# The second layer's down projection in pairs of column tiles, with 6 of its 22 chunk pairs computed by seven block products in place of eight

## What is computed

```
SEQ = 256
D_MODEL = 2048
FFN_HIDDEN = ((-(-8 * D_MODEL // 3)) + 255) // 256 * 256      # 5632
def swiglu(xn, w_gate, w_up, w_down):
    return (jax.nn.silu(xn @ w_gate) * (xn @ w_up)) @ w_down
...
        x = x + swiglu(rms_norm(x, ffn_norm[layer]), w_gate[layer], w_up[layer], w_down[layer])
```

## Time and profile before

| | |
|---|---|
| three executions | 2115.74, 2116.29, 2118.04 us; median 2116.29 |
| the profiled execution: its own time, its span | 2115.71 us, 2113.9 us |
| mean granted TensorE clock, as a share of full speed | 0.999 |
| PE, DVE, ACT busy, share of the span | 100%, 65%, 47% |
| down projection of the second layer, first matmul to first matmul of its second column tile | 59.84 us |

### The profile page before, as it was taken

How to read it: one execution, slowest core, us unless ns; L and a number is a source line. 1 busy time by engine, 2 the same in 40 slices (tenths; PEclk the granted TensorE clock), 3 DMA queues, 4 the chain that set the end, 5 groups by cost and what they waited for, 6 DMA issues and landing times.

```text
span 2113.9 us, 27639 instructions
## 1 busy us (share of the span) xinstructions
PE 2103.6 (100%) x9321; PEld 1739.6 (82%) x9321; DVE 1375.7 (65%) x1879; ACT 996.8 (47%) x1249; POOL 77.5 (4%) x85
## 2 busy tenths in 40 slices
PE   9999999999999999999999999999999999999999
PEld 7788888888888888888888888888888888888887
DVE  5777667676666766565576776676776667664443
ACT  6555555444444444444455565454444444443433
POOL 0110011000000000000011000110000000000000
PEclk9999999999999999999999999999999999999999
DMA  8788666666666665556677774666666666655663
GB/s 277 225 250 254 209 208 199 182 191 199 197 195 181 191 203 182 191 186 207 193 229 248 231 221 152 203 197 198 180 194 202 192 185 189 199 185 201 210 211 136
DMA packets 235252, 427.16 MB, mean 202 GB/s; under 512 B 16176, under 2 KB 37808, under 8 KB 235184
## 3 DMA queue, kind: packets, MB, share of 16 engines
q1 hardware_dynamic: 232736, 422.07, 63.8%
q10 hardware_dynamic: 2448, 4.21, 0.6%
HBM read 410.23 MB, written 15.99 MB: 202 GB/s over the span
## 4 chain that ended last, share of the span: by engine, by line
PE 94%; DVE 2%; DMA 2%; issue 1%; ACT 1%; SPq 0%; POOL 0%; ACTq 0%; DVEq 0%
PE psum L623 30%; PE psum L626 30%; PE psum L624 30%; PE psum L677 1%; PE psum L691 1%; DVE w_lo L1088 1%; DMA block_dram<-turn_sb 1%; DMA w_raw<-in_ab_w_out 1%; DMA w_raw<-in_cd_w_out 1%; PE psum L643 0%; ACT w_hi L777 0%; DVE xt_lo L1164 0%; DMA w_raw<-in_ab_w_in 0%; SPq L509 0%; DMA x_res<-in_x 0%
## 5 line engine op out<-in xcount | busy, mean ns | idle before, releaser
L1088 DVE TENSOR_TENSOR w_lo<-w_raw,w_hi 128x1024 fp32r<-128x1024 f32 x759 | 906.5, 1200 | 619.0 <-ACT w_hi L777 613.5
L777 ACT ACTIVATE w_hi<-w_raw 128x1024 fp32r<-128x1024 f32 x759 | 786.0, 1040 | 933.9 <-PE psum L626 897.4
L623 PE MATMUL psum<-w_hi,xt_hi 128*128 128x512 f32 x2012 | 791.5, 393 | 3.0 <-ACT stage L874 3.0
L626 PE MATMUL psum<-w_hi,xt_lo 128*128 128x512 f32 x2012 | 783.9, 390 | 0.0
L624 PE MATMUL psum<-w_lo,xt_hi 128*128 128x512 f32 x2012 | 783.6, 389 | 0.0
L623 PEld LDWEIGHTS psum<-w_hi,xt_hi 128*128 128x128 f32 x2012 | 378.1, 188 | 81.6 <-DVE w_lo L1088 3.4
L626 PEld LDWEIGHTS psum<-w_hi,xt_lo 128*128 128x128 f32 x2012 | 378.1, 188 | 79.6
L624 PEld LDWEIGHTS psum<-w_lo,xt_hi 128*128 128x128 f32 x2012 | 378.3, 188 | 78.0
L623 PE MATMUL psum<-w_hi,ht_hi 128*128 128x512 f32 x960 | 377.7, 393 | 0.7 <-DVE stage L1121 0.7
L626 PE MATMUL psum<-w_hi,ht_lo 128*128 128x512 f32 x960 | 373.8, 389 | 0.0
L624 PE MATMUL psum<-w_lo,ht_hi 128*128 128x512 f32 x960 | 373.6, 389 | 0.0
(11 more groups left out here) (122 smaller groups left out, 614.9 us busy)
## 6 DMA issues: line engine op xcount, KB each, us to landing
w_raw<-in_w_gate SPq DMA_DIRECT2D x176, 512.0 KB, 3.6
w_raw<-in_w_up SPq DMA_DIRECT2D x176, 512.0 KB, 3.7
w_raw<-in_w_down SPq DMA_DIRECT2D x160, 512.0 KB, 4.1
w_raw<-in_cd_w_in SPq DMA_DIRECT2D x80, 512.0 KB, 4.4
w_raw<-in_ab_w_in SPq DMA_DIRECT2D x71, 512.0 KB, 4.4
w_raw<-in_ab_w_out SPq DMA_DIRECT2D x32, 512.0 KB, 4.2
w_raw<-in_cd_w_out SPq DMA_DIRECT2D x32, 512.0 KB, 3.7
block_dram<-turn_sb SPq DMA_DIRECT2D x18, 512.0 KB, 4.2
```

Source lines behind the costliest of these rows:

```text
L623: nc.tensor.matmul(acc, hi[:, chunk, ts], w_hi[:, slot, c, :], start=first and c == 0, stop=False)
L626: mm = nc.tensor.matmul(acc, lo[:, chunk, ts], w_hi[:, slot, c, :], start=False, stop=end)
L777: nc.scalar.activation(w_hi[:, slot, 0:n, :], w_raw[:, slot, 0:n, :], ACT.Copy).then_inc(hi_ready, 1)
L1088: nc.vector.tensor_tensor(w_lo[:, slot, 0:n, :], w_raw[:, slot, 0:n, :], w_hi[:, slot, 0:n, :].bitcast(F32), ALU.subtract).then_inc(lo_rea ...
```

## The change

The four column tiles of the second layer's down projection become two pairs, the twin tiles (`d` = 0, 1). Within a twin tile the units alternate between the two column tiles `j` = 0 and 1 at the same chunk pair `p`, up to pair 18; the last three pairs come tile by tile. A twin tile has 44 units, and no units of a single chunk are left. The loops over tiles are written out and no longer a hardware loop.

For six of the 22 pairs (`SEVEN`) the four blocks of activations (two token halves by two chunks) and the four blocks of weights (two chunks by two column tiles) are multiplied by the seven products of Strassen's method in Winograd's form. One such group is called **a seven** here. It takes the place of two units, and has 21 matmuls in place of 24. It needs:

- four sums of 128x128 blocks of activations: `row_sums` on DVE (5 operations) into `s_raw`, `rows_hi` on ACT into `s_hi`, and one subtraction on DVE into `s_lo`;
- four sums of 128x512 blocks of weights: 4 operations on DVE in `seven_operands` into `t_raw`, `sums_hi` twice on ACT into `t_hi_sb` (1024 columns each), and two subtractions on DVE into `t_lo_sb`;
- the upper unit (`a`) split as before, and of the lower unit (`b`) only its second chunk (`split_lower` on ACT, and one subtraction of 512 columns on DVE).

Three of the seven products use `w_hi`, `w_lo` or row sums alone (9 matmuls); four use `t_hi_sb` and `t_lo_sb` (12 matmuls), behind one wait for both halves (`tl_ready`). Products that go to one output are accumulated in the tile's own PSUM banks (`plain_bank`), those that go to several in four more banks (`seven_bank`). After the last seven of a twin tile, ACT copies one bank and DVE adds the four banks up with the residual (`combine`, 8 operations); the tile's own banks are added at its end (`output_add`).

```
+PAIRS = HC // 2
+SEVEN = (3, 6, 9, 12, 15, 18)
+PLAIN_END = 19
+TWIN_UNITS = [(j, p) for p in range(PLAIN_END) for j in range(2)]
+TWIN_UNITS += [(j, p) for j in range(2) for p in range(PLAIN_END, PAIRS)]
+TU = len(TWIN_UNITS)
+TWIN_END = [max(i for i, (tile, _) in enumerate(TWIN_UNITS) if tile == j) for j in range(2)]
+SEVEN_END = 2 * SEVEN[-1] + 1
...
+                def three(acc, a_hi, a_lo, b_hi, b_lo, start, stop=False):
+                    nc.tensor.matmul(acc, a_hi, b_hi, start=start, stop=False)
+                    nc.tensor.matmul(acc, a_hi, b_lo, start=False, stop=False)
+                    return nc.tensor.matmul(acc, a_lo, b_hi, start=False, stop=stop)
+                def own(acc, p, c, tok, b_hi, b_lo, start, stop=False):
+                    ts = slice(tok * P, tok * P + P)
+                    return three(acc, ht_hi[:, UC * p + c, ts], ht_lo[:, UC * p + c, ts], b_hi, b_lo, start, stop)
+                def seven_products(d, i, p):
+                    s = len(SEVEN) * d + SEVEN.index(p)
+                    first, last = p == SEVEN[0], p == SEVEN[-1]
+                    a, b = i % RING, (i + 1) % RING
...
+                    pe.wait_ge(lo_ready, twin_unit(d, i) + 1)
+                    own(seven_bank(d, 0), p, 0, 0, w_hi[:, a, 0, :], w_lo[:, a, 0, :], first, last)
+                    mm = own(plain_bank(d, 0, 0), p, 1, 0, w_hi[:, a, 1, :], w_lo[:, a, 1, :], False)
+                    mm.then_inc(unit_used, 1)
+                    pe.wait_ge(lo_ready, twin_unit(d, i + 1) + 1)
+                    pe.wait_ge(s_ready, s + 1)
+                    mm = three(plain_bank(d, 1, 0), s_hi[:, 3, :], s_lo[:, 3, :], w_hi[:, b, 1, :], w_lo[:, b, 1, :], False)
+                    mm.then_inc(unit_used, 1)
+                    pe.wait_ge(tl_ready, 2 * s + 2)
+                    three(seven_bank(d, 1), s_hi[:, 0, :], s_lo[:, 0, :], t_hi_sb[:, 0, :], t_lo_sb[:, 0, :], first, last)
+                    three(seven_bank(d, 3), s_hi[:, 2, :], s_lo[:, 2, :], t_hi_sb[:, 1, :], t_lo_sb[:, 1, :], first, last)
+                    three(seven_bank(d, 2), s_hi[:, 1, :], s_lo[:, 1, :], t_hi_sb[:, 2, :], t_lo_sb[:, 2, :], first, last)
+                    own(plain_bank(d, 0, 1), p, 1, 1, t_hi_sb[:, 3, :], t_lo_sb[:, 3, :], False).then_inc(seven_used, 1)
+                def plain_unit(d, i, j, p):
+                    if p == 0 and j == 0 and d:
+                        pe.wait_ge(combined, d)
+                    pe.wait_ge(lo_ready, twin_unit(d, i) + 1)
+                    for tok in range(TOK):
+                        for c in range(UC):
+                            mm = own(plain_bank(d, j, tok), p, c, tok, w_hi[:, i % RING, c, :], w_lo[:, i % RING, c, :],
+                                     p == 0 and c == 0, i == TWIN_END[j] and c == UC - 1)
...
+                    mm.then_inc(unit_used, 1)
+                if layer == 1:
+                    for d in range(XT // 2):
+                        for i, (j, p) in enumerate(TWIN_UNITS):
+                            if d == 0:
+                                pe.wait_ge(tile_split, split_count(1, "up", p))
+                            if p not in SEVEN:
+                                plain_unit(d, i, j, p)
+                            elif j == 0:
+                                seven_products(d, i, p)
...
+            def split_lower(u, slot):
+                act.wait_ge(w_loaded[slot], loads(u, slot))
+                act.wait_ge(unit_used, u - RING + 1)
+                nc.scalar.activation(w_hi[:, slot, 1, :], w_raw[:, slot, 1, :], ACT.Copy).then_inc(hi_ready, 1)
+            def sums_hi(s, half):
+                if s:
+                    act.wait_ge(seven_used, s)
+                act.wait_ge(t13_summed if half == 0 else t24_summed, s + 1)
+                nc.scalar.activation(t_hi_sb[:, 2 * half:2 * half + 2, :], t_raw[:, 2 * half:2 * half + 2, :],
+                                     ACT.Copy).then_inc(th_ready, 1)
+            def rows_hi(s):
+                if s:
+                    act.wait_ge(seven_used, s)
+                act.wait_ge(s_summed, s + 1)
+                nc.scalar.activation(s_hi[:], s_raw[:], ACT.Copy).then_inc(s_hi_ready, 1)
+            def twin_tiles():
+                for d in range(XT // 2):
+                    for i, (j, p) in enumerate(TWIN_UNITS):
+                        u = twin_unit(d, i)
+                        if p in SEVEN and j == 1:
+                            split_lower(u, i % RING)
+                        else:
+                            split(u, i % RING)
+                        if d == 0 and i == LEAD + 3:
+                            hidden_hi(1, HT - 1)
+                        if p in SEVEN and j == 0:
+                            rows_hi(len(SEVEN) * d + SEVEN.index(p))
+                        for half in range(2):
+                            before = i - 1 - half
+                            if before >= 0 and TWIN_UNITS[before][0] == 1 and TWIN_UNITS[before][1] in SEVEN:
+                                sums_hi(len(SEVEN) * d + SEVEN.index(TWIN_UNITS[before][1]), half)
+                        if i == SEVEN_END + LEAD:
+                            act.wait_ge(seven_used, len(SEVEN) * (d + 1))
+                            if d:
+                                act.wait_ge(x_combined, d)
+                            nc.scalar.activation(stage[2][:, 0, :], seven_bank(d, 0), ACT.Copy).then_inc(p1_copied, 1)
+                        if d == 1 and i in (1, LEAD + 2):
+                            store(0 if i == 1 else 1)
+                store(2)
+                store(3)
...
+            def row_sums(s, p):
+                if s == 0:
+                    dve.wait_ge(unit_used, ph["down", 1]["u"])
+                else:
+                    dve.wait_ge(s_ready, s)
+                dve.wait_ge(tile_split, split_count(1, "up", p))
+                pair = slice(UC * p, UC * p + UC)
+                step.then(nc.vector.tensor_tensor(a_raw[:], ht_hi[:, pair, :].bitcast(F32), ht_lo[:, pair, :].bitcast(F32),
+                                                  ALU.add))
+                a11, a12, a21, a22 = (a_raw[:, c, tok * P:tok * P + P] for tok in range(TOK) for c in range(UC))
+                nc.vector.tensor_tensor(s_raw[:, 2, :], a21, a11, ALU.subtract)
+                step.then(nc.vector.tensor_tensor(s_raw[:, 0, :], a21, a22, ALU.add))
+                step.then(nc.vector.tensor_tensor(s_raw[:, 1, :], s_raw[:, 0, :], a11, ALU.subtract))
+                nc.vector.tensor_tensor(s_raw[:, 3, :], a12, s_raw[:, 1, :], ALU.subtract).then_inc(s_summed, 1)
+            def seven_operands(d, i, p):
+                s = len(SEVEN) * d + SEVEN.index(p)
+                a, b = i % RING, (i + 1) % RING
+                dve.wait_ge(hi_ready, twin_unit(d, i + 1) + 1)
+                if s:
+                    dve.wait_ge(tl_ready, 2 * s)
+                b12, b22 = w_raw[:, b, 0, :], w_raw[:, b, 1, :]
+                nc.vector.tensor_tensor(t_raw[:, 0, :], b12, w_raw[:, a, 0, :], ALU.subtract)
+                nc.vector.tensor_tensor(t_raw[:, 1, :], b12, b22, ALU.subtract).then_inc(t13_summed, 1)
+                dve.wait_ge(t13_summed, s + 1)
+                step.then(nc.vector.tensor_tensor(t_raw[:, 2, :], b22, t_raw[:, 0, :], ALU.subtract))
+                nc.vector.tensor_tensor(t_raw[:, 3, :], w_raw[:, a, 1, :], t_raw[:, 2, :],
+                                        ALU.subtract).then_inc(t24_summed, 1)
+                nc.vector.tensor_tensor(w_lo[:, a, :, :], w_raw[:, a, :, :], w_hi[:, a, :, :].bitcast(F32),
+                                        ALU.subtract).then_inc(lo_ready, 1)
+                nc.vector.tensor_tensor(w_lo[:, b, 1, :], b22, w_hi[:, b, 1, :].bitcast(F32),
+                                        ALU.subtract).then_inc(lo_ready, 1)
+                dve.wait_ge(s_hi_ready, s + 1)
+                nc.vector.tensor_tensor(s_lo[:], s_raw[:], s_hi[:].bitcast(F32), ALU.subtract).then_inc(s_ready, 1)
+                for half in range(2):
+                    dve.wait_ge(th_ready, 2 * s + half + 1)
+                    two = slice(2 * half, 2 * half + 2)
+                    nc.vector.tensor_tensor(t_lo_sb[:, two, :], t_raw[:, two, :], t_hi_sb[:, two, :].bitcast(F32),
+                                            ALU.subtract).then_inc(tl_ready, 1)
+            def combine(d):
...
+                dve.wait_ge(seven_used, len(SEVEN) * (d + 1))
+                dve.wait_ge(x_stored, RES["down", 1] + 1)
+                dve.wait_ge(p1_copied, d + 1)
...
+                dve.wait_ge(combined, d + 1)
+                nc.vector.tensor_tensor(x_res[:, 1, cols(1)], stage[2][:, 0, :], x_res[:, 1, cols(1)],
+                                        ALU.add).then_inc(x_combined, 1)
+            def output_add(n):
+                d, j = n // 2, n % 2
+                dve.wait_ge(x_combined, d + 1)
+                if d:
+                    dve.wait_ge(stored, 3 * 16 * TOK)
```

(56 more changed lines are left out.)

52 lines of the change are left out of this document (37 added, 15 removed).

## The result

| | before | after |
|---|---|---|
| median of 4 runs each on the same chip (lowest to highest) | 2116.11 us (2115.74 to 2118.04) | 2133.88 us (2132.64 to 2134.21) |
| profiled execution: span, mean granted clock | 2113.9 us, 0.999 | 2132.3 us, 0.997 |

The ratio is 1.0085, 95% interval 1.0072 to 1.0098: slower by 17.8 us, against 17 forecast.

A forecast was written before the change was run, and what follows sets the result against it. PE, busy 100% of the span, was taken to bound the kernel. Terms -8.2 + 18.7 + 6.5 = +17.0 on the profiled 2115.71 us gave 2132.7, so a median of 2133 us, range 2122 to 2145.

The forecast's parts named there:

- Removed matmuls, -8.2: On PE, 12 sevens have 36 matmuls fewer, each worth its spacing of 0.2267 us: -8.2 us.
- A steady seven, 1.7 us: PE waits for ACT's split, second copy and DVE's subtraction: 1.7 us per seven, +18.7 us for eleven.
- DVE's row beside it: DVE's sums and subtractions in a steady seven: first half of `t_lo_sb` ends near T + 1.7, before ACT's second copy.
- DVE ends last: Rival: in every seven DVE's operations take 1.0 us more than counted and end after ACT allows: +5, 2138 us; chance 0.12.
- The price of DVE's operations: DVE's SBUF additions of 512 columns priced as subtractions: 0.69 us, starts 0.60 apart unwaited, 0.03 + 0.69 when chained.
- The first seven, +6.5: At the stage's start DVE and ACT still carry the up projection's last tile: PE waits 6.1, restarts and clock added, +6.5 us.
- The twelfth wait on `t_lo_sb`: Expected in the changed profile: twelve PE waits on `t_lo_sb`, eleven of them of 1.3 to 1.7 us idle time.
- Combining and the ends, 0 to 1: After each twin tile's last seven, DVE's adds, some 5.5 us, are hidden: 0 to 0.5 each; tile ends as before.
- every wait costs clock: Rival: each of eleven steady waits lowers PE's clock and costs another 1.6 us: +17.6, 2151 us; chance 0.12.
- My half microsecond: From the earlier trace: no clock fall on PE after half a microsecond of idle time.
- the sums come in time: Rival: at `tl_ready` PE waits less than the break-even 0.68 us per seven; with no wait 2108 us; chance 0.08.

The follow-up runs named there:

- all mended: Changed kernel with ACT's weight-sum copies together, PE's wait in halves, sevens one pair later, `hidden_lo` at the eleventh unit: 2107.47 us against 2114.92 before, ratio 0.9969.
- the twin tiles alone: Changed kernel with every pair computed plainly, without sevens, sums or combining: 2114.95 us against 2114.92 for the kernel before, ratio 1.000.

## Why the prediction was right, step by step

- **Removed matmuls, -8.2:** right. 9285 matmuls are left, and with no wait in the way (all mended) the stage is 7.9 shorter; 0.2 of what is missing lies in its eighth seven. Priced by the 0.39 of one matmul it would have been 14.
- **A steady seven, 1.7 us:** right, 1.68. Each step of its relay is in the rows: copy at T + 1.23 for 1.19, subtraction at 2.30 for 2.28, PE at 3.58 for 3.66. That the sum fits to 0.02 is partly luck: PE went on 0.08 earlier than forecast, and the restart took 0.14 in place of 0.08. That ACT's split, tied to PE's progress, sets it is shown by moving the copy past it: the wait fell to 0.70.
- **DVE's row beside it:** `t_lo_sb`'s first half ended at T + 1.71, as forecast. The rival "DVE ends last" was false for the changed kernel, but by 0.68 us only, and true as soon as ACT's tie is gone.
- **The price of DVE's operations:** the additions of 512 columns in SBUF took 0.68 to 0.69, the 1024 ones 1.22. The Trainium skill ("VectorE: DVE Perf Modes", section "The DRAIN you can't avoid") says, from eight copies in a row, that a semaphore between chained operations costs nothing extra. This case disagrees by a little: the second `t_raw` starts 0.61 behind the first, with no wait between, and the third, which waits for the second, 0.72 behind it. The measurement decides; the sum had 0.72.
- **The first seven, +6.5:** right in mechanism and place (`hidden_hi` at 14.77 after the stage's start for 14.7, DVE at T + 0.66 for 0.65, restart at T + 4.69 for 4.6), too small in one term. I took 0.2 for the clock, because a second wait, for `tl_ready` at T + 8.15, should hide the slow stretch. There was no second wait: with nine matmuls at the slow spacing PE reached that point at T + 8.67, later than the weight sums, which were there at T + 8.0 as forecast. The slow stretch itself, twelve matmuls, became the cost, and the seven measured 7.3. I had counted eight from the earlier trace rows. Nothing in the rows could have told twelve: behind the same wait of 4.53 us five executions have between seven and thirteen, and the seven costs 6.3 to 7.5 (last section). So 6.5 for 7.3 is no error of the mechanism, and how near it came is chance. The twelfth wait on `t_lo_sb` that the forecast lists did not occur.
- **Combining and the ends, 0 to 1:** about 0. The account closes to 0.2 without it, DVE's waits for ACT's two PSUM copies are 0.9 us together and none of PE's waits lies there; for the ends and the written-out loops the twin tiles alone show nothing to pay.
- **Rival "every wait costs clock":** false at 1.38 us of idle time, eleven times out of eleven here and ten out of ten with the first seven left plain; true for eight of eleven at 2.32. It was nearer than the earlier trace rows let me say. My half microsecond from the earlier trace rows was misread too: it is the idle time of the weight loads, and PE's own there is 0.17.
- **Rival "the sums come in time":** false as the kernel stands, and its break-even must be held against the whole cost of a wait, not its idle time: with the copies together the waits are 0.70 but cost 1.0 each with their restarts, 0.3 more than the 0.68 saved. Eleven of these are +3.6, and the first seven adds the larger part of that kernel's loss.

## What to carry to other kernels

Fewer matmuls pay at their spacing and only if every operand is there in time: before anything else, write down for each new operand which engine's in-order queue it stands in and what the instruction ahead of it waits for. Here eleven steady waits cost 18.5 us against a saving of 8.2, and 7.5 of them came from one copy that stood behind a split tied to PE's own progress. Moving that copy by one place, waiting for each half apart and starting one pair later, with `hidden_lo` out of the way, turned +17.8 us into -7.4. A scheme that is put into a steady loop needs its first turn checked by itself, since the stage before still fills the helpers' queues.
